# Route scratch over a gate buffer and two masks, 4 KB a partition more of expert pages loaded ahead of each route, and the first gather by single row blocks

## The reference, cut to what matters

```
h = x
for layer in range(2):
    hn = rmsnorm(h, norm_mix[layer])
    mix = conv_stick_mixer(hn, ...) if layer == 0 else mamba2_mixer(hn, ...)
    h = h + mix
    xt = rmsnorm(h, norm_ffn[layer])
    # group = argmax(softmax(xt @ wg + bg)); the top two of the group's 8 logits are the experts
    # y[token] = sum over its two experts of gate * (silu(xt @ w_gate[e]) * (xt @ w_up[e])) @ w_down[e]
    h = h + y
return rmsnorm(h, final_norm)
```

## Time and profile before

| | |
|---|---|
| median of 3 runs | 1272.65 us (1272.19 to 1274.26) |
| profiled execution | 1272.65 us, span 1270.9 us |
| moved | 461.49 MB, mean 363 GB/s |
| TensorE matmul busy | 1048.5 us, 83% |
| TensorE weight load busy | 712.1 us, 56% |
| VectorE busy | 477.2 us, 38% |
| ScalarE busy | 234.7 us, 18% |
| granted clock of TensorE | 0.903 of full speed |

### The profile page before, as it was taken

The page is one execution under the profiler, slowest core; times in us unless marked ns, Lnnn a source line. Parts: engine busy times, 40 slices in busy tenths (PEclk is TensorE's granted clock), DMA queues, the critical chain, the costliest instruction groups (busy, mean ns, idle before and its releaser), DMA issues.

```text
span 1270.9 us, 22379 instructions
## 1 busy us (share of the span) xinstructions
PE 1048.5 (83%) x9528; PEld 712.1 (56%) x9528; DVE 477.2 (38%) x1227; ACT 234.7 (18%) x526; POOL 4.9 (0%) x27
## 2 busy tenths in 40 slices
PE   9999998966777575799999999998977676758685
PEld 7888755634433342448888888865544343424243
DVE  2342543342223222236665556464344222222232
ACT  2221121111111111113433334121111111111111
POOL 1000000000000000000000000000000000000000
PEclk9999998878788887899999999999898778878799
DMA  9888699999999999995666664999999999999996
GB/s 343 235 336 330 234 422 429 425 429 429 429 429 428 429 429 429 426 392 186 207 216 226 223 215 149 348 344 418 428 428 428 430 428 429 429 428 429 429 426 278
DMA packets 96049, 461.49 MB, mean 363 GB/s; under 512 B 17260, under 2 KB 60520, under 8 KB 70632
## 3 DMA queue, kind: packets, MB, share of 16 engines
q1 hardware_dynamic: 95616, 460.34, 90.1%
q10 hardware_dynamic: 360, 0.15, 0.0%
HBM read 459.38 MB, written 1.08 MB: 362 GB/s over the span
## 4 chain that ended last, share of the span: by engine, by line
PE 55%; DMA 40%; DVE 1%; issue 1%; SPq 1%; ACT 1%; POOL 0%; POOLq 0%; DVEq 0%; ACTq 0%
DMA front<-in_expert_w_up 33%; PE pa L1767 10%; PE pa L1487 10%; PE pb L1487 8%; DMA arena<-in_expert_w_down 5%; PE wa L1767 5%; PE acc L1518 4%; PE wb L1792 3%; PE acc L1625 2%; PE pb L1735 2%; PE acc L1802 1%; PE pb L1551 1%; PE pb L1726 1%; SPq L356 1%; PE pb L1836 1%
## 5 line engine op out<-in xcount | busy, mean ns | idle before, releaser
L1767 PE MATMUL pa<-front,arena 128*32 128x256 f32 x1792 | 137.0, 473 | 90.7 <-DMA front<-in_expert_w_up 90.7
L1767 PEld LDWEIGHTS pa<-front,arena 128*32 128x32 f32 x1792 | 66.7, 135 | 163.4 <-DMA front<-in_expert_w_up 103.2
L1245 DVE TENSOR_SCALAR lower<-lower 128x128 f32<-128x128 f32 x64 | 14.4, 225 | 382.6 <-ACT lower L583 382.6
L1767 PE MATMUL wa<-front,arena 128*32 128x256 f32 x1248 | 93.5, 463 | 64.5 <-DMA front<-in_expert_w_up 60.8
L1767 PEld LDWEIGHTS wa<-front,arena 128*32 128x32 f32 x1248 | 45.6, 132 | 112.8 <-DMA front<-in_expert_w_up 69.6
L583 ACT ACTIVATE arena<-wb 32x256 f32<-32x256 f32 (+2 forms) x236 | 88.9, 377 | 105.6 <-PE wb L1792 96.8
L1792 PE MATMUL wb<-w_dn,conv_raw 128*32 128x256 f32 x1472 | 87.8, 379 | 2.5 <-DMA w_dn<-in_expert_w_down 2.5
L1735 PE MATMUL pb<-arena,hs 128*128 128x128 f32 x448 | 67.6, 313 | 26.0 <-DVE arena L1161 11.3
L1487 PE MATMUL pa<-hnT,w_x 128*128 128x256 f32 x384 | 85.1, 380 | 0.0
L1735 PEld LDWEIGHTS pb<-arena,hs 128*128 128x128 f32 x448 | 61.7, 220 | 40.4 <-DVE arena L1177 18.6
L1487 PEld LDWEIGHTS pa<-hnT,w_x 128*128 128x128 f32 x384 | 72.5, 190 | 10.0 <-issue 0.3
(11 more groups left out here) (340 smaller groups left out, 1219.8 us busy)
## 6 DMA issues: line engine op xcount, KB each, us to landing
w_dn<-in_expert_w_down SPq DMA_DIRECT2D x46, 2048.0 KB, 26.0
front<-in_expert_w_gate SPq DMA_DIRECT2D x42, 2048.0 KB, 19.0
front<-in_expert_w_up SPq DMA_DIRECT2D x42, 2048.0 KB, 23.4
w_x<-in_expert_w_gate SPq DMA_DIRECT2D x15, 2048.0 KB, 30.3
w_x<-in_expert_w_up SPq DMA_DIRECT2D x15, 2048.0 KB, 34.6
arena<-in_expert_w_down SPq DMA_DIRECT2D x14, 2048.0 KB, 26.5
w_x<-in_odd_in_proj SPq DMA_DIRECT2D x16, 1024.0 KB, 5.4
front<-in_expert_w_up SPq DMA_DIRECT2D x8, 1024.0 KB, 9.3
```

Source lines behind the costliest of these rows:

```text
L1245: link(v.tensor_scalar(eg, eg, 1.0, None, ALU.add))
L1767: ins = mm(gu[32 * j:32 * j + 32, :, :], xb[:, k, c0:c0 + CAP], w[k][:, :, P * j:P * j + P], start=(k == 0), stop=(k == KC - 1))
```

## The change

**Scratch.** The mask of the route lies in `strict` and the logits in `lower`, the rest of the scratch in `arena` over the rows that later hold the positions and gates (from 7*NE on). So arena from 2*CHUNK on is free during the route and holds expert 0's row block 5 (`sixth0`). Because the table for the selection of rows lies there as well, VectorE waits for expert 0's `gu_done` ahead of the first `select_rows`.

**Pages.** Row block 4 stays in chunk 4, now in its first half (`fifth0`). The second half takes row blocks 2 and 3 of the gate matrix of expert 4 ahead of the route (half of a quarter, 512 KB); what is left of the quarter is issued once block 4 of expert 0 has been used. SP has five more DMAs a layer.

**First gather.** `gather_first` and `gathered_first` go by one row block: eight gathers, eight evictions of 128x128 (a tensor_scalar with a per-partition scalar in place of tensor_tensor), put between the steps of the route at eight places; gate/up by one block.

**Ranks.** 1000 is added to the diagonal of `upper`, so that a masked rank is 1000 higher; `iota1` and `slot_id` start at 1001. `select_quad(0)` reads the ranks from PSUM ahead of the product with the mask. The scan of layer 1 needs the plain `upper`, so the 1000 is taken off in layer 0 behind expert 7 and put on again ahead of layer 1's route.

**Small ones.** `even_norm` makes the mean square of each half ahead of the copy of that half; `warm(7)` is `warm(4)`.

```diff
@@ buffers
-        early0 = chunks(2, 3).rearrange("p (a g k f) -> p a g k f", a=3, g=2, k=2)
+        early0 = chunks(2, 2).rearrange("p (a g k f) -> p a g k f", a=2, g=2, k=2)
+        fifth0 = chunks(4, 1)[:, 0:2 * FF].rearrange("p (g f) -> p g f", g=2)
+        sixth0 = arena[:, 2 * CHUNK:2 * CHUNK + 2 * FF].rearrange("p (g f) -> p g f", g=2)
-        first_used = [2 * CHUNK, DN3]
+        first_used = [7 * NE, 7 * NE + 2 * SEQ]
-        mask, lg = take_route(TT, NE), take_route(TT, NG + NE)
+        mask = strict[:, 0:TT * NE].rearrange("p (t e) -> p t e", t=TT)
+        lg = lower[:, 0:TT * (NG + NE)].rearrange("p (t e) -> p t e", t=TT)
@@ SP, layer 0 (layer 1: the same loads at the places of first_pages and first_last)
             quarter(0, 3, 1, 0, "gu_in0")
+            first_rows(0, fifth0, 4, 5)
+            quarter(0, 4, 0, 0, "gu_in1", 2, 4)
...
-            first_last(0)
+            first_rows(0, last0, 6, 8)
             expert_part(0, 3, 2, half=1)
+            sp_.wait_ge(S["conv_done"], EVEN_UNITS)
+            first_rows(0, sixth0, 5, 6)
@@ SP, behind expert 0's row blocks
-                quarter(l, 4, 0, 0, "gu_in1")
+                quarter(l, 4, 0, 0, "gu_in1", 0, 2)
@@ VectorE
+            def raise_diagonal(by):
+                link(v.scalar_tensor_tensor(upper[:, :], ident[:, :], float(by), upper[:, :], ALU.mult, ALU.add))
...
+                select_quad(0, prk)
                 v.tensor_tensor(pos, prk, mask, ALU.mult).then_inc(S["mask_done"], 1)
                 dve.wait_ge(S["mask_done"], 2 * l + 2)
-                select_quad(0)
...
                 link(v.scalar_tensor_tensor(s1, e2, 1.0, gs, ALU.add, ALU.mult))
+                gathered_first(l, 0)
                 link(v.reciprocal(g1, s1))
                 link(v.tensor_tensor(g2, g1, e2, ALU.mult))
-                gathered_first(l, 0)
+                gathered_first(l, 1)
...
                 link(v.tensor_tensor(cols2, over(other), along(cols[:, :, WIDE:WIDE + 1]), ALU.mult))
+                gathered_first(l, 6)
                 link(v.tensor_tensor(cols, cols, over(keep), ALU.mult))
                 link(v.tensor_tensor(cols, cols, cols2, ALU.add))
                 link(v.tensor_tensor(cols2, over(here), along(at_other[:, 0:6].unsqueeze(2)), ALU.mult))
+                gathered_first(l, 7)
                 link(v.tensor_tensor(cols, cols, cols2, ALU.add))
...
-            def gathered_first(l, part):
-                dve.wait_ge(S["gath_done"], PARTS * l + part + 1)
-                k = slice(2 * part, 2 * part + 2)
-                v.tensor_tensor(xs[:, k, :], (XG, XG1)[part % 2][:, 0:2, :],
-                                nffn[:, l, k].unsqueeze(2).to_broadcast([P, 2, QUAD * CAP]), ALU.mult
+            def gathered_first(l, k):
+                dve.wait_ge(S["gath_done"], PARTS * l + k + 1)
+                v.tensor_scalar(xs[:, k, :], (XG, XG1)[k % 2][:, 0, :], nffn[:, l, k:k + 1], None, ALU.mult
                                 ).then_inc(S["xs_done"], 1)
@@ TensorE
             def first_gate_up(l):
                 gather_first(l, 0)
                 gather_first(l, 1)
-                for part in range(FIRST):
-                    if 0 < part < FIRST - 1:
-                        gather_first(l, part + 1)
-                    pe.wait_ge(S["xs_done"], PARTS * l + part + 1)
-                    ins = gate_up(xs, 0, early_cols(0), GU[0], ks=(2 * part, 2 * part + 1))
-                    if part < FIRST - 1:
+                pe.wait_ge(S["mask_done"], 2 * l + 2)
+                for k in range(KC):
+                    if 0 < k < KC - 1:
+                        gather_first(l, k + 1)
+                    pe.wait_ge(S["xs_done"], PARTS * l + k + 1)
+                    ins = gate_up(xs, 0, early_cols(0), GU[0], ks=(k,))
+                    if k in (1, 3, 4):
                         ins.then_inc(S["gu_half"], 1)
...
-                    warm(7)
+                    warm(4)
```

More of the change, by code:

```diff
@@ L36 @@
 FIRST = 4
-PARTS = FIRST + 2 * (NE // QUAD - 1)
+PARTS = KC + 2 * (NE // QUAD - 1)
 LISTED = 8
+FAR = 1000
 OV_AT = 27
@@ L513, in _ @@
                         quarter(1, 3, 1, 0, "gu_in0")
+                        first_rows(1, fifth0, 4, 5)
+                        quarter(1, 4, 0, 0, "gu_in1", 2, 4)
                 else:
@@ L556, in _ @@
             for q in range(4):
-                chain.link(nc.gpsimd.iota(slot_id[32 * q:32 * q + 32, :], pattern=[[0, 1]], base=1,
+                chain.link(nc.gpsimd.iota(slot_id[32 * q:32 * q + 32, :], pattern=[[0, 1]], base=FAR + 1,
                                           channel_multiplier=1, allow_small_or_imprecise_dtypes=True))
@@ L911, in even_norm, with mean @@
                 v.tensor_copy(norm_w[:, :, :].rearrange("p a k -> p (a k)"), acc[:, 3, 256:288]).then_inc(S["norm_cols"], 1)
-                for t in range(TT):
-                    dve.wait_ge(S["x_t"], t + 1)
-                    v.tensor_copy(resT[:, 4 * t:4 * t + 4, 0:P], (pa, pb)[t][:, :].rearrange("p (k m) -> p k m", k=4)
-                                  ).then_inc(S["x_raw_dve"], 1)
+                def mean(t):
                     dve.wait_ge(S["x_sq"], t + 1)
@@ L918, in even_norm, with turned_in @@
                                     ).then_inc(S["mean_sq"], 1)
+                def turned_in(i):
+                    dve.wait_ge(S["x_t"], i + 1)
+                    v.tensor_copy(resT[:, 4 * i:4 * i + 4, 0:P], (pa, pb)[i][:, :].rearrange("p (k m) -> p k m", k=4)
+                                  ).then_inc(S["x_raw_dve"], 1)
+                mean(0)
+                turned_in(0)
+                mean(1)
+                turned_in(1)
                 dve.wait_ge(S["norm_cols"], 1)
@@ L1148, in select_rows, with select_quad @@
                                     [NE, 1, QUAD, CAP]), 1.0, None, ALU.mult).then_inc(S["prep_sel"], 1)
-            def select_quad(q):
+            def select_quad(q, ranks=pos):
                 v.tensor_tensor(quad_slots.rearrange("p t (e s) -> p t e s", e=QUAD),
                                 iota1[:, :].unsqueeze(1).unsqueeze(1).to_broadcast([P, TT, QUAD, CAP]),
-                                pos[:, :, ds(q * QUAD, QUAD)].unsqueeze(3).to_broadcast([P, TT, QUAD, CAP]),
+                                ranks[:, :, ds(q * QUAD, QUAD)].unsqueeze(3).to_broadcast([P, TT, QUAD, CAP]),
                                 ALU.is_equal).then_inc(S["quad_sel"], 1)
             def gathered(q, l, half):
-                dve.wait_ge(S["gath_done"], PARTS * l + FIRST + 2 * (q - 1) + half + 1)
+                dve.wait_ge(S["gath_done"], PARTS * l + KC + 2 * (q - 1) + half + 1)
                 k = slice(KC // 2 * half, KC // 2 * half + KC // 2)
@@ L1237, in moe @@
                     E = NE * l + e
+                    if e == 0:
+                        dve.wait_ge(S["gu_done"], NE * l + 1)
                     if e < NE - 2:
@@ L1276, in moe @@
                         gathered(q + 1, l, 1)
+                    if l == 0 and e == LISTED - 1:
+                        raise_diagonal(-FAR)
                     if e == LISTED:
@@ L1731, in gather_quad @@
                     pe.wait_ge(S["g4_done"], NE * l + QUAD * q)
-                pe.wait_ge(S["xs_done"], PARTS * l + FIRST + 2 * (q - 1) + half)
+                pe.wait_ge(S["xs_done"], PARTS * l + KC + 2 * (q - 1) + half)
                 for k in range(KC // 2):
@@ L1743, in early_cols @@
                 if e == 0:
-                    return [early0[:, k // 2, :, k % 2, :] for k in range(KC - 2)] + [last0[:, :, k, :] for k in range(2)]
+                    return ([early0[:, k // 2, :, k % 2, :] for k in range(4)] + [fifth0, sixth0]
+                            + [last0[:, :, k, :] for k in range(2)])
                 return [early1[:, k // 2, :, k % 2, :] for k in range(KC)]
@@ L1748, in late_cols, with gather_first @@
                 return [(late3, late4)[e - 3][:, k // 4, :, k % 4, :] for k in range(KC)]
-            def gather_first(l, part):
-                if part == 0:
+            def gather_first(l, k):
+                if k == 0:
                     pe.wait_ge(S["quad_sel"], NE // QUAD * l + 1)
                     pe.wait_ge(S["hs_done"], 4 * l + 4)
-                if part > 1:
-                    pe.wait_ge(S["xs_done"], PARTS * l + part - 1)
-                for k in (2 * part, 2 * part + 1):
-                    for t in range(TT):
-                        ins = mm((XG, XG1)[part % 2][:, k % 2, :], hs[:, t, k, :], quad_slots[:, t, :],
-                                 start=(t == 0), stop=(t == TT - 1))
+                if k > 1:
+                    pe.wait_ge(S["xs_done"], PARTS * l + k - 1)
+                for t in range(TT):
+                    ins = mm((XG, XG1)[k % 2][:, 0, :], hs[:, t, k, :], quad_slots[:, t, :],
+                             start=(t == 0), stop=(t == TT - 1))
                 ins.then_inc(S["gath_done"], 1)
@@ L1876, in middle_quad @@
```

(4 more changed lines are left out.)

29 lines of the change are left out of this document (17 added, 12 removed).

## The result

| kernel | median of its runs, us | runs | against before |
| --- | --- | --- | --- |
| before | 1273.29 (1271.67 to 1275.05) | 8 | |
| after | 1279.12 (1275.18 to 1281.90) | 8 | 1.0043, 95% interval 1.0029 to 1.0058 |

The change makes the kernel 0.43% slower, some 5.5 us. The prediction had the sign and most of the mechanism, but its 2.0 us are less than half of it, and 1279.1 lies outside its range (1270.5 to 1276.9).

The account below looks back on a forecast made before the run. It took TensorE's chain from route to expert 4 to set when expert 6's weights are issued, with the DMA queue running dry. +1.3 +1.35 -0.55 -0.15, plus 0.05 for loose ends, gave +2.0 us: 1274.7, range 1270.5 to 1276.9.

Parts of the forecast that it names:

- The route's first step: Quad 0's slots read the ranks straight from PSUM, so the first gather starts 0.26 us earlier.
- TensorE's changes: Expert 0's switches between gather (0.20 us each) and gate/up (0.14): four more of each, 1.36 us more.
- VectorE's side: Expert 0's eight evictions, the last behind the column swap, make its last gate/up block end 1.65 us late.
- The upper bound of 2.0: Upper bound on expert 0's lateness in us, with 0.05 more for each added wait; 1.65 was taken.
- The stream behind the refill runs as from 187.46, 1.3 late: Layer 0's transfers behind expert 6's first gate-matrix issue run 1.3 us late; layer 1's 1.35.
- the credit: Bytes still queued before the change at expert 6's first issue, 0.67 and 0.50 MB, 1.56 and 1.16 us of transfer.
- The base, -1.85: Streams 0.6 and 0.55 us earlier in layers 0 and 1, with 0.7 more: -1.85 us, 1270.8.
- rival C: Expert 0's route ends 0.26 us earlier, changes cost nothing and evictions keep up: 1270.8 us, chance 0.10.
- the start's 0.15: At the kernel's start, the mean of x's second half no longer waits for the second PSUM copy: 0.15 us earlier.
- The warming matmuls: Ahead of layer 1, seven warming matmuls become four: 0.55 us earlier.
- Rival B: Bytes loaded ahead of the route count in full, 1.22 us a layer saved: 1269.5 us, chance 0.13.
- Rival D: The forecast plus a wait of up to 2.2 us in layer 1's mixer for a projection chunk: 1276.9 us, chance 0.12.

Follow-up runs that it names:

- The delay: The pairs kernel with nine matmuls on zeros ahead of expert 0's last pair of gate/up blocks, both layers: 1277.17 us, 1.0029 of before.
- the bank: Quad 1's gather in two PSUM banks: on the pairs kernel 1271.19 us (0.9983), that without the loads ahead 1270.23 (0.9975), on the changed kernel 1271.58 (0.9985).
- the pairs runs: The changed kernel with expert 0 gathering pairs of row blocks again, four evictions at the old places, run twice: 1274.16 us (0.9997) and 1273.08 us (0.9994).
- the first profile of after: The changed kernel's first profiled execution, 1281.23 us, with TensorE's clock at 1.2 GHz for some microseconds in layer 0.
- halves: The pairs kernel with expert 0 gathered in two halves of four row blocks, two evictions of 128x512: 1273.09 us, 0.9989; with evictions on ScalarE 1274.63 us, 1.0004.
- the second profile of after: The changed kernel run again unchanged: 1278.64 us, 1.0033 of before; its profiled execution took 1276.24 us.
- the run without the loads ahead: The pairs kernel with the 4 KB a partition loaded behind the route again, scratch in its old place: 1273.03 us, 0.9988 of before.
- the sixth block's run: The changed kernel with layer 1's sixth row block issued behind expert 2's and 3's down matrices instead of ahead: 1279.06 us, 1.0034 of before.

## Why the prediction was wrong in size

**Where the loss is.** Right: expert 0's evictions behind the column swap, TensorE late, the queue dry at the refill. The delay, the bank and the pairs runs each confirm a link of that.

**The route's first step, 0.26 us earlier.** Right: in the first profile of after, everything lies 1.09 us late ahead of the route (its start took longer) and only 0.83 at the first gather. **TensorE's changes.** Right: 0.64 a gather between blocks and 0.57 a gate/up block (twice that is 0.19 above a pair's 1.09 and 0.14 above its 1.00), and halves take 7.40 against 8.07, 0.67 less, where 2 x 0.20 + 2 x 0.14 were to fall away.

***VectorE's side*, "1.65 us late".** Mis-sized. The first eviction starts 0.80 us behind the first gather, as forecast; the eighth comes 8.51 behind the first where 8.26 were forecast, and the last block ends 1.05 behind its start where 0.91 were (its own parts, 154.58 + 0.43 + 0.1, give 0.04 less). That makes 10.36 - 8.06 - 0.26 = 2.04 us late in layer 1, 1.89 in the second profile's layer 0 (10.22 - 8.07 - 0.26), together 0.63 more than 2 x 1.65. The upper bound of 2.0 (0.05 more for each added wait) was the better value, and the last gate/up block took 0.64 us. The estimate of 0.291 us for 128 elements, from the formula of the Trainium skill (VectorE: DVE Perf Modes, the section on the TRN2 errata), is for another operation, a tensor_tensor. These take 0.35 each, and let the next one start after 0.27.

**"The stream behind the refill runs as from 187.46, 1.3 late".** This step failed by as much. I took 0.35 and 0.30 us off the delays for what the queue still held before the change (0.67 and 0.50 MB). The runs show no such credit: the last down matrix lands 382.7 to 383.9 us behind the refill in the four layers of before that were profiled, and 382.9 to 384.6 in the four of after. If the credit were there, after would lie 0.3 lower; on the mean it lies 0.2 higher, with a scatter larger than either. So the delay is to be counted in full from 38.7 us on, 0.65 more for both layers. Between pairs and blocks the sum had no credit: both ran from a dry queue, 1.91 us a layer apart. (The expectation of the delay run, that by the sum 0.8 of a delay reaches the end, misreads it; 0.8 is the share against before.) With 2.29 us more for expert 0 than pairs in layer 1 (10.36 - 8.07) and 2.15 in layer 0, it is 4.4 us, where the sum had 2 x 1.91 = 3.8.

**The base, -1.85.** By the same sum the change with pairs (rival C's state) should have come to 1270.8; it measured 0.4 to 0.8 us under before. What didn't come: the start's 0.15 (the first V projection starts at 9.18 to 9.68 us in most profiles of the changed start, at 9.38 and 9.36 before), and at least the credit's part of the earlier refills' 0.6 and 0.55 (in the second pairs profile expert 4's gate/up ends at 183.64, 0.34 earlier, and layer 0's last down matrix still lands at 567.60 instead of 567.22). **The warming matmuls** came as forecast. In the first profile after:

```profile
574.31 0.04 issue
...
577.07 0.97 PE pa L1512 x4
578.04 0.12 issue
578.16 0.38 PE wb L2031
```

From the last landing to layer 1's first matmul are 3.85 us where there were 4.38, 0.53 less.

**The sum again**, with what was measured: pairs -0.6, blocks +4.4, so 3.8 us where 4.2 and 5.5 were measured in two series. So the mechanism was right and three of its terms were mis-sized: VectorE's side (0.63), the credit for the queue (0.65) and the start (0.15). With them the forecast's 2.0 becomes 3.4; what is missing up to 4.2 and 5.5 is not explained. **Rival B** (the bytes count) falls by the run without the loads ahead, in a stronger form than I had: not even with a full queue at the refill was a gain seen. **Rival C** falls with expert 0's 10.36 us. **Rival D** fell with the sixth block's run. Of the tests named beforehand, TensorE does wait for VectorE ahead of its last block, and the refill comes 40.8 to 41.0 us behind the first gather (40.6 forecast). Expert 0's 10.2 to 10.4 us lie above the 9.7 to 10. The hole is there, but not empty: in the second profile of after the weakest microsecond at the refill moves 115 GB/s in either layer; only the first profile, with the clock fallen, has two with 0 and 16. The chance given to a slower kernel was too small (0.30), since two choices, the credit for the queue and the 1.65 between its bounds, both leaned to the mild side.

**What stays open.** The changed kernel lies 1.0033 and 1.0043, single blocks alone on the kernel before 1.0026, the pure delay 1.0029. Whether up to 1 us or so more is lost when both parts meet can't be told within the intervals. How much of the 2.0 to 2.3 us is TensorE's changes and how much the late evictions was not split cleanly either: with the evictions earlier or on another engine expert 0 took 9.71 and 9.67 us, which leaves 1.6 us for TensorE and 0.5 to 0.7 for VectorE, but the times moved by other amounts than these. Why ScalarE's evictions gave back 3 to 4 us instead of 1.3 is not settled either; VectorE's relief behind expert 0 is only a guess.

## What to carry to other kernels

Ask of each refill how much the queue still holds when it is issued. If next to nothing, what lengthens the compute chain up to it lengthens the whole by as much, and bytes moved away ahead of it saved nothing here; if the queue holds some, a longer chain (up to that much) or a finer split costs little. Here two freed waits of 1 us in quad 1's gather turned the changed kernel's loss of 4 to 5 us into a gain of 2 against before, and brought 3 with pairs and without the loads ahead. How much of it is the earlier refill and how much the clock was not told apart.

When work is cut finer and put between the steps of another list, price the changes between kinds of work and, above all, what the last piece stands behind. Then look at what waits for the end of that list, since pulling the pieces up moved the wait there.

## What the runs showed of the hardware

TensorE's granted clock fell to 0.50 (1.2 GHz) for a few microseconds between expert 0 and expert 4 in 13 of the 28 layers profiled without the last edit, in before as in after, in quad 1's gather or in the wait of 1.08 us ahead of it: its sixteen matmuls took 2.6 to 3.75 us instead of 2.02. It fell in 5 of 12 layers with single blocks and in 8 of 16 without them (pairs, halves, the kernel before), so no tie to the change is seen. In the six layers with the edit, where that wait is gone, it fell only behind expert 4's gate/up, where TensorE waits for weights anyway. So some of that edit's gain may be the clock's; it was not told apart. It moves the refill by up to 2.8 us in a layer. That fits the spread of one kernel's executions: before spreads over 6.7 us (35 executions) beside three kernels with that edit that spread over 2.1 to 4.3 (eleven or twelve each). The mean clock of an execution (0.894 to 0.908, the one of 3128.72 us apart) tells little. A single profile's difference of a few microseconds says nothing without the clock of each stretch.

In four of the 17 profiles (the first of after, the halves, the delay and the pairs with two banks) the start's sixteen transposes took 0.85 us for four instead of 0.44, although the row shows a granted clock of 1.00:

```profile
5.00:9.00 4.00, 3.58 (x18) 3.48 (x18) 1.80 (x9) 2.31 (x5) 1.10 (x2) 1.00 1.08 357
```

The first projection then starts 1 us or more later (10.45 us in the first profile of after, 9.41 in the second). No edit goes with it.
